# Two gates' seven half-size products in another order: the second gate's first ones in the first tile, the first gate's last ones in the second

## The reference

```python
proj = x @ lp['w_in']
cq, ckv, kr, f_pre, q_pre, i_pre, g_pre, ga, gb = jnp.split(proj, ...)
...
o = o * jax.nn.silu(g_pre.astype(jnp.float32)).reshape(B, L, HG_HEADS, HG_DV)
...
merged = jax.nn.sigmoid(ga) * (a @ lp['w_br_a']) + jax.nn.sigmoid(gb) * (o @ lp['w_br_b'])
x = layernorm(DN_ALPHA * x + merged @ lp['w_out'], lp['ln1_g'], lp['ln1_b'])
x = layernorm(DN_ALPHA * x + hier_moe(x) + ple_term, lp['ln2_g'], lp['ln2_b'])
```

## Time and profile before

| | |
|---|---|
| median of 3 runs | 1526.13 us (1526.11 to 1533.0) |
| profiled execution, its own time | 1530.24 us |
| its span, first to last instruction | 1528.5 us |
| PE busy | 1272.7 us, 83% of the span |
| PEld (weight loads, beside PE) | 739.2 us, 48% |
| DVE busy | 436.2 us, 29% |
| ACT busy | 284.1 us, 19% |
| POOL busy | 71.3 us, 5% |
| mean granted PE clock | 0.913 of 2.4 GHz |
| HBM | 492.87 MB read, 2.89 MB written |

### The profile page before, as it was taken

One profiled execution on the slowest core, in us unless ns is written; L12 is line 12 of the kernel. 1 busy time (PEld: TensorE's weight loads), 2 busy tenths in 40 slices (PEclk: granted clock), 3 DMA queues, 4 the chain that ended last, 5 costly groups with the idle time before them and its releaser, 6 DMA issues.

```text
span 1528.5 us, 21258 instructions
## 1 busy us (share of the span) xinstructions
PE 1272.7 (83%) x8912; PEld 739.2 (48%) x8913; DVE 436.2 (29%) x1101; ACT 284.1 (19%) x712; POOL 71.3 (5%) x110
## 2 busy tenths in 40 slices
PE   7999899999787767767799998999996787677665
PEld 4767897554332323322266678976352323223211
DVE  4242753542111101001143547445311111011003
ACT  3343422021001101000044434211111011010001
POOL 1301000000000000000022011000000000000000
PEclk9999999999898877778899999999998988778888
DMA  9505966989999999999972079669999999999994
GB/s 332 164 1 152 255 168 225 399 355 429 430 428 429 430 431 429 431 429 428 379 255 84 3 198 297 180 229 417 378 429 431 431 429 430 430 430 430 429 425 173
DMA packets 85330, 505.60 MB, mean 331 GB/s; under 512 B 7600, under 2 KB 13680, under 8 KB 54128
## 3 DMA queue, kind: packets, MB, share of 16 engines
q1 hardware_dynamic: 75392, 476.47, 75.9%
q0 software_dynamic: 9840, 27.71, 8.4%
HBM read 492.87 MB, written 2.89 MB: 324 GB/s over the span
## 4 chain that ended last, share of the span: by engine, by line
PE 55%; DMA 35%; DVE 4%; SPq 3%; ACT 1%; issue 1%; POOL 0%; DVEq 0%
PE bank L1109 53%; DMA ring<-in_w_e_up 7%; DMA ring<-in_w_e_down 5%; DMA ring<-in_w_e_gate 5%; DMA arena<-in_w_e_up 4%; DMA arena<-in_w_e_gate 4%; DMA cst<-in_w_e_down 4%; DMA cst<-in_w_e_gate 3%; DMA arena<-in_w_e_down 2%; PE bank L1159 2%; SPq L921 2%; DMA ring<-in_w_in 1%; SPq L982 0%; DVE cst L2333 0%; DVE arena L2337 0%
## 5 line engine op out<-in xcount | busy, mean ns | idle before, releaser
L1109 PE MATMUL bank<-arena 128*32 128x512 f32 (+11 forms) x2808 | 568.5, 537 | 175.7 <-DMA ring<-in_w_e_up 48.7
L1109 PE MATMUL bank<-ring,arena 128*32 128x512 f32 (+4 forms) x1360 | 416.9, 646 | 36.4 <-DMA arena<-in_w_e_gate 18.7
L1109 PEld LDWEIGHTS bank<-arena 128*32 128x32 f32 (+6 forms) x2808 | 208.5, 137 | 436.4 <-issue 423.7
L1109 PE MATMUL bank<-ring,xT 128*32 128x128 f32 (+5 forms) x1536 | 237.3, 364 | 1.3 <-ACT xT L1728 1.1
L1109 PEld LDWEIGHTS bank<-ring,xT 128*32 128x32 f32 (+1 forms) x1536 | 121.5, 137 | 100.7 <-issue 90.2
L1109 PEld LDWEIGHTS bank<-ring,arena 128*32 128x32 f32 (+1 forms) x1360 | 107.0, 130 | 126.7 <-issue 119.8
L1109 PE MATMUL bank<-xT,ring 128*128 128x144 f32 (+1 forms) x640 | 111.8, 335 | 0.0
L1109 PEld LDWEIGHTS bank<-xT,ring 128*128 128x128 f32 x640 | 96.2, 190 | 13.6
L1109 PE MATMUL bank<-arena,x_sb 128*128 128x128 f32 (+1 forms) x768 | 99.7, 282 | 1.4 <-DVE arena L2496 0.8
L1109 PEld LDWEIGHTS bank<-arena,x_sb 128*128 128x128 f32 (+1 forms) x768 | 90.5, 190 | 19.4 <-issue 12.7
L1109 PE MATMUL bank<-cst,arena 128*32 128x512 f32 x144 | 82.7, 728 | 0.0
(11 more groups left out here) (250 smaller groups left out, 1008.4 us busy)
## 6 DMA issues: line engine op xcount, KB each, us to landing
arena<-in_w_e_up SPq DMA_DIRECT2D x30, 2048.0 KB, 28.9
arena<-in_w_e_gate SPq DMA_DIRECT2D x28, 2048.0 KB, 27.7
ring<-in_w_e_gate SPq DMA_DIRECT2D x24, 2048.0 KB, 25.6
arena<-in_w_e_down SPq DMA_DIRECT2D x20, 2048.0 KB, 23.0
ring<-in_w_e_down SPq DMA_DIRECT2D x18, 2048.0 KB, 24.3
ring<-in_w_in SPq DMA_DIRECT2D x32, 1024.0 KB, 9.5
ring<-in_w_e_up SPq DMA_DIRECT2D x16, 2048.0 KB, 25.0
arena<-in_w_e_gate SPq DMA_DIRECT2D x16, 1024.0 KB, 14.4
```

The source lines that it names most:

```text
L1109: return pe.matmul(out, lhsT, rhs, start=first, stop=last, skip_group_check=True)
```

## The change

Three things are changed. The order of a gate's products becomes 4, 5, 3, 2, 1, 6, 7 (it was 4, 5, 3, 2, 7, 1, 6). At the three late places of tile 0, where a7, a1 and a6 stood, stand b4, b5 and b3 now; at the three of tile 1 where these stood, stand a1, a6 and a7. And of a gate's weight sums, the one for product 2 goes out first and the one for product 7 last, so that POOL waits for the sum of product 6 before it. The weight quarters are loaded in the order (0,0), (1,1), (1,0), (0,1), and ACT's last sigmoid waits for product 7 in place of 1.

```diff
-SEVEN = (4, 5, 3, 2, 7, 1, 6)
+SEVEN = (4, 5, 3, 2, 1, 6, 7)
...
-           ("A", 0, 1): seven_of("ga", 2), ("A", 0, 3): seven_of("ga", 7), ("ks", 0): seven_of("ga", 1), ("o", 0): seven_of("ga", 6),
-           ("A", 1, 1): seven_of("gb", 4), ("A", 1, 3): seven_of("gb", 5), ("ks", 1): seven_of("gb", 3), ("o", 1): seven_of("gb", 2),
-           ("A", 2, 0): seven_of("gb", 7, 1), ("ks", 2): seven_of("gb", 6)}
+           ("A", 0, 1): seven_of("ga", 2), ("A", 0, 3): seven_of("gb", 4), ("ks", 0): seven_of("gb", 5), ("o", 0): seven_of("gb", 3),
+           ("A", 1, 1): seven_of("ga", 1), ("A", 1, 3): seven_of("ga", 6), ("ks", 1): seven_of("ga", 7), ("o", 1): seven_of("gb", 2),
+           ("A", 2, 0): seven_of("gb", 1, 6), ("ks", 2): seven_of("gb", 7)}
...
-    out += [(name, j, h) for name in ("ga", "gb") for j in range(2) for h in range(2)]
+    out += [(name, j, h) for name in ("ga", "gb") for j, h in ((0, 0), (1, 1), (1, 0), (0, 1))]
...
-                    pool.wait_ge(ring_full[SIGNAL_OF[ns[0, 1]]], 16 * FILLS[ns[0, 1]])
-                    pool.dma_start(w[0, 1], from_input(1, 1), accum_op=ALU.add).then_inc(half_sum[7], 16)
                     job_done(pool, (layer, name, 4, 1))
...
                     pool.dma_start(w[1, 0], w[1, 1], accum_op=ALU.add).then_inc(half_sum[6], 16)
+                    pool.wait_ge(ring_full[SIGNAL_OF[ns[0, 1]]], 16 * FILLS[ns[0, 1]])
+                    pool.wait_ge(half_sum[6], summed_halves(layer, name))
+                    pool.dma_start(w[0, 1], from_input(1, 1), accum_op=ALU.add).then_inc(half_sum[7], 16)
...
-                        job_read(act, (layer, "ga" if k < 4 else "gb", 6 if k // 2 % 2 else 1, k % 2))
+                        job_read(act, (layer, "ga" if k < 4 else "gb", 6 if k // 2 % 2 else 7, k % 2))
```

## The result

| | before | changed |
|---|---|---|
| median of 7 runs | 1527.06 us | 1535.22 us |
| lowest and highest | 1526.11 and 1533.0 us | 1532.98 and 1537.78 us |
| profiled execution, span | 1530.24 us, 1528.5 us | 1534.55 us, 1532.8 us |

The ratio is 1.0045, with a 95% interval from 1.0030 to 1.0061. The forecast was 4.8 us more than before, 1531; the first ratio says 6.9, the second 9.8. The direction and nearly all places are right, the size is short by 2 to 5 us, and the median of 1535.22 lies above the 1529 to 1533 that I gave for my own case.

The account below looks back on a forecast made before the run. DVE's chain sets the stage; PE's eight gaps, 10.4 us, are the most the change can take. Delays of 1.7 us in layer 0 and 3.1 in layer 1 make +4.8 on the median 1526.13: 1531 us, range 1529 to 1533.

Parts of the forecast that it names:

- my own case: Whole kernel: the forecast's main case, 4.8 us slower, 1531 us, range 1529 to 1533; chance 0.43.
- Starts of the products: Layer 0, tiles 0 and 1: b3 starts 1.09 us sooner, the squares 2.71 later, a6 0.98 later than b5 did.
- a7, b6 and the remainder: Tiles 1 and 2: a7's place 1.4 us late, b6 and the remainder of the layer 1.7 us late.
- Sums and weights: POOL's weight sums and SP's weight loads: sums land before use, product 2's first is worth nothing, loads taken at nothing.
- The clock: Layer 1: a slow stretch of the granted clock falls on b3 and adds 1.4 us, making 3.1 for the layer.
- the forecast's last sentence: Whole kernel: what would make the time wrong is foremost a slow stretch of the clock that falls elsewhere.
- the clock as well: Rival: a slow stretch follows the new gap ahead of a6, 1.4 to 1.7 us each, 1534 with both layers; chance 0.20.
- A delay of this stage goes to the end undiminished: Recurrence to kernel end: all delay stays, since the experts' transfers into the arena wait for the merged gates.
- The table load: ACT's Silu block: its table loads take 1.28 us each without a drain, the block 4.26 us.
- The rival with a drain: ACT's Silu block: a drain follows each table load, so the block takes 7.0 us, 1536.5 in all; chance 0.02.

Follow-up runs that it names:

- e1: The changed kernel with ACT's Silu block of the output gate moved ahead of its two copies of b3; ratio 1.0011 to the kernel before.
- e8: The changed kernel with products that nobody reads in both idle times, eight ahead of b3 and seven ahead of a6; ratio 1.0008 to the kernel before.
- e3: The changed kernel with POOL's old order of the shared sums, product 7's half first; ratio 1.0042 to the kernel before.
- e6: The changed kernel with the Silu block ahead of b3's copies and eight unread products in the idle time ahead of b3; ratio 0.9981 to the kernel before.
- e4: The changed kernel with seven unread products in PE's idle time ahead of a6; ratio 1.0042 to the kernel before.
- after_again: The changed kernel measured once more, unaltered, with a profile of its own; ratio 1.0064 to the kernel before.
- e2: The kernel before with one wait added: ACT's Silu block waits for the second part of a6; ratio 1.0001 to the kernel before.
- e9: The kernel before with five unread products in PE's idle time ahead of a1; ratio 1.0009 to the kernel before.
- e5: The changed kernel with the Silu block ahead of b3's copies and DVE's additions of b5 ahead of tile 0's last placing; ratio 0.9979 to the kernel before.

## Why the forecast was right in kind and short in size

**Starts of the products.** Right. By the forecast, then as measured, the whole stage being 0.13 earlier (169.07 for 169.20): b5 177.4 and 177.17, b3 184.03 and 183.89, end of its copies 188.65 and 188.49, squares 192.91 and 192.78, line 2414 194.65 and 194.52, a6 200.65 and 200.52. The chain from DVE's freed bank over ACT's copies, the table loads, the squares and DVE's additions back to PE is thereby shown link by link, and e1 shows the cause: with the block ahead of the copies a6's idle time goes.

**a7, b6 and the remainder.** Right, where b3 and a6 run at full speed. In e8 a7's place stands 38.14 us behind b4 (206.56 - 168.42), for 36.83 before: 1.3 late, forecast 1.4. b6 is 1.64 late (54.71 for 53.07), forecast 1.7. The first `bra` product is 1.63 late, forecast 1.7. In the changed kernel's own first trace it is 4.4 late in layer 0 and 1.6 in layer 1, where 1.7 and 3.1 were forecast: the clock's term fell in the other layer, and on another product.

**Sums and weights.** Right: e3 and the rows of b4.

**The clock.** This is the term of the sum that was mis-sized, and the forecast's last sentence had named it as the one that could be. I gave it 1.4 us, on b3 in layer 1 alone. In the first profile it was nothing there and 3.0 us on a6 in layer 0 (7.0 for 4.0); in the second 1.67 on b3 in both layers and 1.6 on a6. I had taken one trace's slow stretch as fixed to one place, and had put the new idle time ahead of a6 among the rivals as though the two excluded each other. What the rows ahead of the prediction held, and I didn't use: in layer 0 the idle time ahead of a1 was short only because a7 had run slowly, while a7 to a6 was the same in both layers. So the long idle time, and the term, belonged in either layer. In the traces here b3 was slow in nine of the eleven cases in which it stood behind 2.5 to 3.8 us of idle time without a filling. By e1 against e6 its stretch is worth 4.6 us in the two layers, by e4 against after_again a6's is worth 3.3. The measured time is nearer to the rival "the clock as well", at 1534, than to my own case.

**"A delay of this stage goes to the end undiminished".** This step failed in two comparisons: in e8, and here. In the first pair of profiles the stage is 4.41 + 1.63 = 6.04 us longer and the span 4.3. Most of the difference is given back at the end of layer 0's experts. The tensor engine's timeline there, first of the kernel before, then of the changed one:

```profile
755.92 0.62 PE L1109 MATMUL bank<-arena 128*32 128x512 f32 x1 [3.09 <-DMA arena<-in_w_e_down]
...
758.02 5.67 PE L1109 MATMUL bank<-arena 128*32 128x512 f32 x25
764.96 1.32 PE L1159 MATMUL bank<-cst,x_sb 128*128 128x128 f32 x8 [1.26 <-DVE x_sb L2141]
```

```profile
760.35 0.62 PE L1110 MATMUL bank<-arena 128*32 128x512 f32 x1 [2.18 <-DMA arena<-in_w_e_down]
...
761.68 4.82 PE L1110 MATMUL bank<-arena 128*32 128x512 f32 x25
767.76 1.32 PE L1160 MATMUL bank<-cst,x_sb 128*128 128x128 f32 x8 [1.26 <-DVE x_sb L2142]
```

The first row of each is the matmul that waits for the last expert weights, the second the 25 that end the experts, the third the transposes of the next layer. From the landing to the transposes it is 9.04 us before and 7.41 after. The granted clock was 0.79 before (756 to 764 us), behind 3.09 us of idle time, and 1.00 after (760.3 to 767), behind 2.18. So 1.63 us come back, by the clock. The stretch takes 9.03 to 9.04 us in the three traces of the old order (before, e2, e9), and of the nine with the changed order 7.41 to 7.42 in seven, 8.76 in e8 and 9.04 in e5. The length of the idle time doesn't decide it: after_again waited 3.09 us here too and took 7.42. Whether the changed stage makes it so, or chance, isn't settled: no run here changes the end of the experts alone.

It doesn't explain e8 either, whose stretch is only 0.28 us shorter than before's. e8's trace is also 1.5 us shorter from the first `bra` product to the landing, and 1.5 from layer 1's first `bra` product to the end, but over the twelve traces these two lengths lie 2.2 and 2.1 us apart, so one trace of it shows no cause. Against the step's failing stands e1 against e6: 4.4 us of the stage, and 4.6 of the time.

With both corrections the first pair of profiles comes out: 6.04 - 1.63 = 4.4 us, for 4.3 in the span. For the times most is the slow stretches of b3 and a6: the filling of e8 takes 5.6 of the 6.9 us away (1.0045 to 1.0008), or 8.6 by the second measurement, and leaves 1.2. That is more than the 2.8 and 4.8 us of slow stretches that the stage shows in the two profiles of the changed kernel, so a remainder of some 3 to 4 us stays unexplained (the second profile is of the fastest of its five runs, 2.0 us below their median).

**The table load.** The rival with a drain is refuted by the ACT rows above. The rows ahead of the prediction could not show it at the second load, whose end at 188.20 was followed by a wait for PE until 190.20; in the changed kernel the squares start 0.02 us behind it (191.48 + 1.28, and 192.78).

## What to carry to other kernels

Follow a moved product through every engine that must read it before its bank is free, and look at what stands behind those reads in the same queue: two copies of 0.4 us ahead of a 4.3 us block that could have run during the wait made the stage 1.6 us longer. With the block ahead of them the order shows a gain, once b3's idle time is filled (e6, 0.9981) or shortened (e5, 0.9979). When a change joins two short idle times of the tensor engine to a long one, add a slow stretch behind it as a likely cost in every layer where it stands, and ask whether anything waits for the end of that product; where nothing does, as in the old order, it is free as far as the idle time behind it reaches. Useless products in an idle time are a cheap test of whether the clock is to blame.

## What the runs showed of the hardware that was not expected

Where a slow stretch falls differs between executions of one program: in the same kernel b3 took 4.16 and 5.83 us behind 3.78 us of idle time, and a6 4.0 to 7.0 behind 1.9. In e1 b3 ran at a granted clock of 0.60 for 7.0 us, and with eight useless products ahead of it (e6) at 1.00. That made 0.3% of the whole kernel, from about 2 us a layer of matmuls that nobody reads.
